# Three ring banks for the turned blocks of an attention stage, turns ahead of scores on TensorE, and the lambda rows taken last

## The chip, the cores and the metric

The kernel runs on one NeuronCore of one Trainium2 chip. The metric is the device time of one launch in microseconds (us), the median of several runs. Engines are named as in the profile: PE is TensorE, DVE is VectorE, ACT is ScalarE, POOL is GpSimd, and SP issues DMAs.

## The reference

One inference step of a two-layer hybrid backbone in float32, for 128 context tokens and 512 latent tokens. Each layer mixes tokens in three groups of heads (a gated DeltaNet, grouped-query attention, differential attention), projects the result, and runs a feed-forward part (dense in layer 0, a mixture of experts in layer 1). The change touches only the attention of the two layers:

```python
# B: 6 query heads, 2 key heads, 64 wide; latent queries see cached and latent keys, context queries see context keys
p = softmax(q_b @ k_b.T * HEAD_DIM ** -0.5);  o_b = p @ v_b
# C: 4 heads, two 32-wide softmax maps each, 64-wide values
p = softmax(q_c[m] @ k_c[m].T * DIFF_HD ** -0.5)          # m = 0, 1
lam = exp(sum(lv[0] * lv[1])) - exp(sum(lv[2] * lv[3])) + lam_init
o_c = rmsnorm((p[0] - lam * p[1]) @ v_c, diff_norm) * (1 - lam_init)
```

## The kernel before

The program is a row of stages; in each stage every engine has an instruction list written out by hand, and the engines meet at semaphores. At a stage's end all engines wait for one another. The change is in `attention`, called once for each of the two layers. It has two stages.

**The prepare stage** splits queries and keys into a high and a low part and transposes them, for seven items (five new tiles, two cached ones). For an item n, ACT writes the high parts (`split_hi`, L1567 to L1572), DVE the low parts (`split_lo`, L1518 to L1524), PE transposes them (L1602 to L1613), and ACT and DVE bring the results out of PSUM (`bring_out`). The rows of lambda, `lv`, arrive by SP's first DMA of the stage. DVE multiplies and sums them (L1539, L1540) before its first `split_lo`; ACT takes their exponential (L1588) after its first `split_hi`. Meanwhile POOL squares the DeltaNet output, five operations (L1503).

**The softmax stage** works through 14 units: six heads of kind B and four heads of kind C with two maps m = 0, 1 each. All loops over units are software-pipelined: iteration v issues work of unit v (`now`), of v+1 (`ahead`) and of v-1 (`done`). A unit has five query tiles t (tile 0 is the context). For each tile:

- **S**t: `scores` on PE into one of two pairs of banks (0 and 1, 2 and 3). Kind B takes four matmuls, kind C two, tile 0 a quarter of that.
- **least** on DVE (L1836, a reduction over the scores in PSUM), then **exp** on ACT (L1903, in the list `probabilities`), which frees the score banks for the scores after the next.

The probabilities are transposed in seven blocks (`ITEMS`), **T**0 to **T**6 (`turn`, L1743, four 128x128 transposes each, T3 only one). Each lands in a bank of the ring; ACT copies it out as the high part (**hi**j, L1913), DVE subtracts for the low part (**lo**j, L1841), and after that the bank is free. Then **W** (`weigh`, L1761) multiplies two key blocks by the values: W of the first half (tiles 1, 2) waits for lo2, that of the second half (tiles 3, 4) for lo6 and runs in the next iteration. **X** (`weigh_context`, L1772) does the context tile. ACT brings the sums out (L1921, L1923), **R** (`turn_out`, L1782) transposes them back on PE, and DVE scales them (**out**, L1847 to L1857; maps m = 1 have two more operations there than m = 0).

Waits that matter: S waits until exp has read the tile two before; T waits for lo of the block that last held its bank; W0 for lo2 or lo6; DVE does, in order, lo0, least1, lo1, least2, lo2, lo3, lo4, least3, lo5, least4, out, lo6, least0, and the change leaves this order and ACT's as they are in this stage. Before the change the PSUM banks are: ring 4 and 5, the sums in 6, and bank 7 for both X's result and R's result:

```python
RING, OB, XB = 4, 6, 7
def ring(n): return ps[:, RING + n % 2, :]
```

In layer 0 SP also fills 25 MB of slots with zeros during this stage.

Of the kernel before, what the change touches and what calls it, by code (L numbers as in the profile page):

```python
# [25 lines left out]
P = 128  # L26
# [129 lines left out]
class Kernel:  # L156
# [1264 lines left out]
    def attention(self, l):  # L1421
# [12 lines left out]
        with ExitStack() as scope:  # L1434
# [12 lines left out]
            with ExitStack() as inner:  # L1447
# [33 lines left out]
                with stage(nc, names) as (block, s):  # L1481
# [26 lines left out]
                    def _(dve):  # L1508
# [27 lines left out]

                        dve.wait_ge(s["lv_in"], 16)
# [3 lines left out]
                        for n in range(len(items)):  # L1541
                            split_lo(n)
                            if n:
                                bring_out(n - 1)
# [11 lines left out]
                    def _(act):  # L1556
# [30 lines left out]
                        act.wait_ge(s["lsum"], 1)  # L1587
                        act.activation(ls[:], ls[:], ACT.Exp).then_inc(s["lexp"], 1)  # L1588
# [3 lines left out]
                        bring_out(len(items) - 1)  # L1592

# [46 lines left out]
            RING, OB, XB = 4, 6, 7  # L1640
# [11 lines left out]
            def ring(n):  # L1652
                return ps[:, RING + n % 2, :]
# [11 lines left out]
            def turned(n):  # L1665
                size = len(ITEMS[n % NS])
                if size == 1:
                    return ring(n)[:, 0:P]
                return ring(n).rearrange("p (k q) -> p k q", k=4 if ITEMS[n % NS][0][1] == 0 else 2)
# [15 lines left out]
            with stage(nc, "folded v_hi v_lo scores least p_in turned hi lo pv pvc o_sb o_ctx o_turned o_out chain zeroed filled root inv gated") as (block, s):  # L1685
# [29 lines left out]
                def _(pe):  # L1715
# [21 lines left out]
                    def turn(u, j):  # L1737
                        n = NS * u + j
                        pe.wait_ge(s["p_in"], max(order(u, t) for t, k in ITEMS[j]) + 1)
                        if n >= 2:  # L1740
                            pe.wait_ge(s["lo"], n - 1)
                        for q, (t, k) in enumerate(ITEMS[j]):
                            mm = pe.transpose(ring(n)[:, q * P:(q + 1) * P], prob_block(u, t, k) if t else prob_slot(u, 0), self.ident)  # L1743
# [22 lines left out]
                    def weigh_context(u):  # L1766

                        pe.wait_ge(s["lo"], NS * u + 4)
                        if u:
                            pe.wait_ge(s["o_out"], u)  # L1770
                        for n, part in enumerate((p_hi, p_lo)):
                            mm = pe.matmul(ps[:, XB, 0:P], values(u, 0), part[:, PL:PL + P], start=(n == 0), stop=(n == 1))  # L1772
                        mm.then_inc(s["pvc"], 1)

                    def turn_out(u):
# [4 lines left out]
                        pe.wait_ge(s["o_ctx"], u + 1)  # L1780
                        for t in range(NT):
                            mm = pe.matmul(ps[:, XB, P + t * HD:P + (t + 1) * HD], oT[:, (t - 1) * P:t * P] if t else oTc, fold,  # L1782
                                           start=True, stop=True)
                        mm.then_inc(s["o_turned"], 1)
                    for v in range(-1, NU + 1):
                        ahead, now, done = v + 1 < NU, 0 <= v < NU, v >= 1
                        if ahead:
                            scores(v + 1, 1)
# [992 lines left out]
```

## Time and profile before

| | |
|---|---|
| median of 3 runs | 2812.03 us (2804.58 to 2816.2) |
| the profiled execution | 2805.11 us, of it the span of instructions 2803.4 us |
| busy in the span | PE 2426.6 us (87%), DVE 1450.3 us (52%), ACT 1068.4 us (38%) |
| prepare stage, layer 0 | 411.1 to 447.3 us |
| softmax stage, layer 0 | 447.3 to 652.1 us |
| softmax stage, layer 1 | 1617.7 to 1819.2 us |
| ACT's copies L1913, all 196: idle before them | 122.5 us, for PE's turns L1743 |
| DVE's subtractions L1841, all 196: idle before them | 117.9 us, for ACT's copies L1913 |

A row of a timeline gives the start in us, the duration in us, the engine, the line, the operation and its operands, how many instructions are merged in the row, and in brackets the idle time of the engine before it with what ended it. Two instructions of one engine overlap slightly in such rows, so what an instruction costs its engine in a full queue is the distance to the next start.

### The profile page before, as it was taken

How to read it: one execution, taken by the hardware profiler on the slowest of the kernel's cores; microseconds unless marked ns; L12 is line 12 of the kernel's file. 1: busy time of each engine (PE TensorE's matmuls, PEld its weight loads, DVE VectorE, ACT ScalarE, POOL GpSimd, SP SyncE). 2: the span in 40 equal slices, each digit the busy share in tenths (PEclk: the TensorE clock that was granted, in tenths of full speed). 3: DMA queues.
4: the chain of work that ended last, by engine and by line, in shares of the span. 5: the costliest groups of instructions: out<-in, count | busy, mean ns of one | idle time of the engine just before them, and what ended most of it. 6: DMA issues, size and time to landing. Idle time of an engine off the chain costs nothing. (4 is left out here: it accounts for less than half of the span.)

```text
span 2803.4 us, 47191 instructions
## 1 busy us (share of the span) xinstructions
PE 2426.6 (87%) x19308; PEld 2197.1 (78%) x19308; DVE 1450.3 (52%) x2079; ACT 1068.4 (38%) x1752; POOL 312.2 (11%) x334
## 2 busy tenths in 40 slices
PE   5996777877899999989958688784799999999993
PEld 4984555667899999989846656684799999999992
DVE  5576555575422322346746646642454555555456
ACT  4332235563422112243322456622344444444443
POOL 0055232000000000000643220001000000000002
PEclk8998887999999999999979889995899999999997
DMA  5233666502222322223157000011866676676654
GB/s 209 84 82 76 198 187 204 171 1 73 64 76 57 87 76 66 62 53 90 41 115 204 23 1 1 3 59 61 253 205 179 209 229 192 186 224 209 188 183 175
DMA packets 453116, 340.49 MB, mean 121 GB/s; under 512 B 90961, under 2 KB 421151, under 8 KB 451935
## 3 DMA queue, kind: packets, MB, share of 16 engines
q1 hardware_dynamic: 436383, 277.43, 34.3%
q10 hardware_dynamic: 11520, 41.95, 4.6%
q0 software_dynamic: 5056, 18.88, 1.7%
q8 instruction: 116, 1.90, 0.3%
q14 instruction: 41, 0.34, 0.0%
HBM read 287.68 MB, written 50.53 MB: 121 GB/s over the span
## 5 line engine op out<-in xcount | busy, mean ns | idle before, releaser
L2346 PE MATMUL ps<-h_hi,w_hi 128*128 128x256 f32 x1408 | 400.1, 284 | 5.5 <-DVE w_lo L2429 5.5
L2346 PE MATMUL ps<-h_lo,w_hi 128*128 128x256 f32 x1408 | 399.5, 284 | 0.0
L2346 PE MATMUL ps<-h_hi,w_lo 128*128 128x256 f32 x1408 | 399.5, 284 | 0.0
L2429 DVE TENSOR_TENSOR w_lo<-w_raw,w_hi 128x2048 fp32r<-128x2048 f32 (+1 forms) x180 | 309.2, 1756 | 120.5 <-ACT w_hi L2379 120.5
L2346 PEld LDWEIGHTS ps<-h_hi,w_hi 128*128 128x128 f32 x1408 | 271.2, 193 | 8.7 <-issue 5.9
L2346 PEld LDWEIGHTS ps<-h_lo,w_hi 128*128 128x128 f32 x1408 | 271.2, 193 | 2.8
L2346 PEld LDWEIGHTS ps<-h_hi,w_lo 128*128 128x128 f32 x1408 | 271.1, 193 | 0.0
L2379 ACT CAST w_hi<-w_raw 128x2048 fp32r<-128x2048 f32 (+1 forms) x180 | 256.4, 1473 | 2.6 <-DMA w_raw<-in_moe_w_down 2.6
L1841 DVE TENSOR_TENSOR p_lo<-ps,p_hi 128x512 fp32r<-128x512 f32 (+1 forms) x196 | 123.6, 632 | 123.0 <-ACT p_hi L1913 117.9
L2648 PE MATMUL ps<-ffn_h_hi,w_hi_ffn 128*128 128x320 f32 x704 | 161.5, 311 | 5.6 <-DVE ffn_h_lo L378 4.2
L2648 PE MATMUL ps<-ffn_h_lo,w_hi_ffn 128*128 128x320 f32 x704 | 160.9, 310 | 0.0
L2648 PE MATMUL ps<-ffn_h_hi,w_lo_ffn 128*128 128x320 f32 x704 | 160.9, 310 | 0.0
L2391 ACT ACTIVATE silu_g<-ps 128x256 f32<-128x256 f32 x88 | 33.8, 384 | 326.2 <-PE ps L2346 326.1
L1913 ACT CAST p_hi<-ps 128x512 fp32r<-128x512 f32 (+1 forms) x196 | 106.4, 544 | 122.5 <-PE ps L1743 122.5
L2439 DVE TENSOR_TENSOR silu_g<-silu_g,ps 128x256 f32<-128x256 f32 x88 | 37.0, 421 | 194.1 <-ACT silu_g L2391 194.1
L1743 PE MATMUL ps<-cst,tm 128*128 128x128 f32 x700 | 116.3, 287 | 12.0 <-DVE p_lo L1841 12.0
L596 PE MATMUL ps<-w_hi_in,h_hi 128*128 128x454 f32 x320 | 122.4, 382 | 4.6 <-DVE w_lo_in L152 3.1
L2648 PEld LDWEIGHTS ps<-ffn_h_hi,w_hi_ffn 128*128 128x128 f32 x704 | 118.4, 189 | 7.0 <-issue 6.7
L2092 DVE SCALAR_TENSOR_TENSOR xT<-ps,mod,xT 128x128 f32<-128x128 f32 (+2 forms) x96 | 36.3, 434 | 168.9 <-PE ps L2659 104.3
L1903 ACT ACTIVATE tm<-ps,tm 128x768 f32<-128x768 f32 (+1 forms) x140 | 111.7, 798 | 30.8 <-DVE tm L1836 30.8
L1836 DVE TENSOR_REDUCE tm<-ps 128x1 f32<-128x768 f32 (+1 forms) x140 | 114.0, 816 | 17.5 <-PE ps L1731 17.3
L596 PE MATMUL ps<-w_lo_in,h_hi 128*128 128x454 f32 x320 | 119.4, 373 | 0.0
(426 smaller groups left out, 5603.9 us busy)
## 6 DMA issues: line engine op xcount, KB each, us to landing
w_raw<-in_moe_w_gu SPq DMA_DIRECT2D x182, 512.0 KB
w_raw<-in_moe_w_down SPq DMA_DIRECT2D x91, 512.0 KB
G_decay<-in_ada_w ACTq DMA_DIRECT2D x54, 512.0 KB, 4.7
w_ahead<-in_ffn_w_gu SPq DMA_DIRECT2D x44, 512.0 KB, 5.3
slots_h<-tm SPq DMA_DIRECT2D x13, 1024.0 KB, 11.2
slots_y<-tm SPq DMA_DIRECT2D x12, 1024.0 KB, 11.4
w_ahead<-in_ffn_w_down SPq DMA_DIRECT2D x16, 704.0 KB, 4.7
oA<-in_ada_w ACTq DMA_DIRECT2D x20, 512.0 KB, 5.2
```

What stands on the lines that cost most here:

```text
L596: mm = pe.matmul(ps[:, t, 0:TMT], x[:, 4 * half + k, t * P:(t + 1) * P], wt[:, tile % 2, k * TMT:(k + 1) * TMT], start=(half == 0 and k == ...
L1743: mm = pe.transpose(ring(n)[:, q * P:(q + 1) * P], prob_block(u, t, k) if t else prob_slot(u, 0), self.ident)
L1836: dve.tensor_reduce(low[:, u % 2, t:t + 1], score_tile(u, t), AX.X, ALU.min).then_inc(s["least"], 1)
L1841: dve.tensor_tensor(place(p_lo, j), turned(n), place(p_hi, j).bitcast(F32), ALU.subtract).then_inc(s["lo"], 1)
L1903: act.activation(prob_slot(u, t), x.rearrange("p (a n) -> p a n", a=3) if t else x, ACT.Exp, scale=-1.0, bias=low[:, u % 2, t:t + 1], accu ...
L1913: act.copy(place(p_hi, j), turned(n)).then_inc(s["hi"], 1)
L2092: dve.scalar_tensor_tensor(out=x, in0=self.ps[:, 2 * (m % 4) + half, a - a0:b - a0], scalar=self.mod[:, l, gate, m, j:j + 1], in1=x, op0=A ...
L2346: mm = pe.matmul(ps[:, j % 2, half * BLK:(half + 1) * BLK], gu(wt, j, half, k), x[:, k, :], start=(k == 0 and n == 0), stop=(k == KC - 1 a ...
L2379: act.copy(whi[:, q, part], raw[:, q, part]).then_inc(s["hi_d" if down else "hi_u"], 1)
L2429: dve.tensor_tensor(wlo[:, q, part], raw[:, q, part], whi[:, q, part].bitcast(F32), ALU.subtract).then_inc(s["lo_d" if down else "lo_u"], 1)
L2439: dve.tensor_tensor(g, g, ps[:, j % 2, BLK:2 * BLK], ALU.mult).then_inc(s["prod"], 1)
L2648: mm = pe.matmul(ps[:, 4 * (j % 2) + 2 * half + st, 0:b - a], wt[:, u, o:o + P], x[:, k, a:b], start=(k == 0 and m == 0), stop=(k == KC - ...
```

## The change

In the prepare stage DVE's two products and the sum of the lambda rows move from the front of its list to behind the last `split_lo`, and ACT's exponential moves behind the last `bring_out`. In the softmax stage the ring has three banks (4, 5, 6), X's and R's results get no bank of their own but take turns in the ring, and the sums move to bank 7. The ring's order in a unit is T0, T1, T2, X, T3, T4, T5, R, T6 over the banks 0, 1, 2, 0, 1, 2, 0, 1, 2. On PE, S1 moves behind T0 and the W that follows it, S2 behind T2, S3 behind T4 and its W, and S4 behind R.

```diff
@@ prepare stage, DVE @@
+                        for n in range(len(items)):
+                            split_lo(n)
+                            if n:
+                                bring_out(n - 1)
                         dve.wait_ge(s["lv_in"], 16)
                         for j in range(2):
                             chain(dve.tensor_tensor(lp[:, j], lv[:, 2 * j], lv[:, 2 * j + 1], ALU.mult))
                         dve.tensor_reduce(ls[:], lp[:], AX.X, ALU.add).then_inc(s["lsum"], 1)
-                        for n in range(len(items)):
-                            split_lo(n)
-                            if n:
-                                bring_out(n - 1)
                         bring_out(len(items) - 1)
...
@@ prepare stage, ACT @@
                         split_hi(0)
-                        act.wait_ge(s["lsum"], 1)
-                        act.activation(ls[:], ls[:], ACT.Exp).then_inc(s["lexp"], 1)
                         for n in range(1, len(items)):
                             split_hi(n)
                             bring_out(n - 1)
                         bring_out(len(items) - 1)
+                        act.wait_ge(s["lsum"], 1)
+                        act.activation(ls[:], ls[:], ACT.Exp).then_inc(s["lexp"], 1)
...
@@ softmax stage @@
-            RING, OB, XB = 4, 6, 7
+            RING, OB = 4, 7
...
-            def ring(n):
-                return ps[:, RING + n % 2, :]
+            BANK = {0: 0, 1: 1, 2: 2, "context": 0, 3: 1, 4: 2, 5: 0, "result": 1, 6: 2}
+
+            def ring(j):
+                return ps[:, RING + BANK[j], :]
...
                     def turn(u, j):
-                        n = NS * u + j
                         pe.wait_ge(s["p_in"], max(order(u, t) for t, k in ITEMS[j]) + 1)
-                        if n >= 2:
-                            pe.wait_ge(s["lo"], n - 1)
+                        if j == 0 and u:
+                            pe.wait_ge(s["lo"], NS * (u - 1) + 6)
+                        elif j == 1 and u:
+                            pe.wait_ge(s["lo"], NS * (u - 1) + 4)
+                            if u >= 2:
+                                pe.wait_ge(s["o_out"], u - 1)
+                        elif j == 2 and u:
+                            pe.wait_ge(s["lo"], NS * u)
+                        elif j == 5:
+                            pe.wait_ge(s["lo"], NS * u + 1)
+                            if u:
+                                pe.wait_ge(s["o_ctx"], u)
+                        elif j >= 3:
+                            pe.wait_ge(s["lo"], NS * u + {3: 2, 4: 3, 6: 5}[j])
...
                     def weigh_context(u):
 
-                        pe.wait_ge(s["lo"], NS * u + 4)
-                        if u:
-                            pe.wait_ge(s["o_out"], u)
+                        pe.wait_ge(s["lo"], NS * (u + 1) + 1 if u + 1 < NU else NS * NU)
...
                         pe.wait_ge(s["o_ctx"], u + 1)
+                        if u + 1 < NU:
+                            pe.wait_ge(s["lo"], NS * (u + 1) + 4)
+                        else:
+                            pe.wait_ge(s["o_out"], u)
...
                     for v in range(-1, NU + 1):
                         ahead, now, done = v + 1 < NU, 0 <= v < NU, v >= 1
-                        if ahead:
-                            scores(v + 1, 1)
                         if now:
                             turn(v, 0)
                         if done:
                             weigh(v - 1, 1, 0)
                             weigh(v - 1, 1, 1)
+                        if ahead:
+                            scores(v + 1, 1)
                         if now:
                             turn(v, 1)
-                        if ahead:
-                            scores(v + 1, 2)
...
                             turn(v, 2)
+                        if ahead:
+                            scores(v + 1, 2)
...
                             turn(v, 3)
+                            turn(v, 4)
+                            weigh(v, 0, 0)
+                            weigh(v, 0, 1)
                         if ahead:
                             scores(v + 1, 3)
                         if now:
-                            turn(v, 4)
-                            weigh(v, 0, 0)
-                            weigh(v, 0, 1)
                             turn(v, 5)
-                        if ahead:
-                            scores(v + 1, 4)
-                        if now:
                             weigh(v, 0, 2)
                             weigh(v, 0, 3)
                         if done:
                             turn_out(v - 1)
+                        if ahead:
+                            scores(v + 1, 4)
```

Where PE's list passes from one unit of kind C to the next, before the change: S0 (128 keys), S1 (512 and 256 keys), T0 (the transposes of `cst,tm`), the first four matmuls W, T1.

```order
L1734 MATMUL ps<-kC,qC 128x128
L1734 MATMUL ps<-kC,qC 128x512
L1734 MATMUL ps<-kC,qC 128x256
L1743 MATMUL ps<-cst,tm 128x128 x4
L1761 MATMUL ps<-p_hi,vC 128x256
L1761 MATMUL ps<-p_lo,vC 128x256
L1761 MATMUL ps<-p_hi,vC 128x256
L1761 MATMUL ps<-p_lo,vC 128x256
L1743 MATMUL ps<-cst,tm 128x128 x4
```

The same place of PE's list in the changed kernel (the line numbers are its own):

```order
L1735 MATMUL ps<-kC,qC 128x128
L1755 MATMUL ps<-cst,tm 128x128 x4
L1773 MATMUL ps<-p_hi,vC 128x256
L1773 MATMUL ps<-p_lo,vC 128x256
L1773 MATMUL ps<-p_hi,vC 128x256
L1773 MATMUL ps<-p_lo,vC 128x256
L1735 MATMUL ps<-kC,qC 128x512
L1735 MATMUL ps<-kC,qC 128x256
L1755 MATMUL ps<-cst,tm 128x128 x4
```

S1 has moved behind T0 and the W whose first matmul waits for lo6 of the unit before.

PE's list from T5 to T6 in a unit of kind C, before the change: T5, S4, four matmuls W, R (x5), T6.

```order
L1743 MATMUL ps<-cst,tm 128x128 x4
L1734 MATMUL ps<-kC,qC 128x512
L1734 MATMUL ps<-kC,qC 128x256
L1761 MATMUL ps<-p_hi,vC 128x256
L1761 MATMUL ps<-p_lo,vC 128x256
L1761 MATMUL ps<-p_hi,vC 128x256
L1761 MATMUL ps<-p_lo,vC 128x256
L1782 MATMUL ps<-tm 128x64 x5
L1743 MATMUL ps<-cst,tm 128x128 x4
```

The same place in the changed kernel:

```order
L1755 MATMUL ps<-cst,tm 128x128 x4
L1773 MATMUL ps<-p_hi,vC 128x256
L1773 MATMUL ps<-p_lo,vC 128x256
L1773 MATMUL ps<-p_hi,vC 128x256
L1773 MATMUL ps<-p_lo,vC 128x256
L1796 MATMUL ps<-tm 128x64 x5
L1735 MATMUL ps<-kC,qC 128x512
L1735 MATMUL ps<-kC,qC 128x256
L1755 MATMUL ps<-cst,tm 128x128 x4
```

S4 has moved behind the W and behind R.

DVE's list at the start of the prepare stage, the change against before; `lp` and `ls` are the products and sums of lambda:

```order
 L1507 UNCONDITIONAL_BRANCH
-L1539 TENSOR_TENSOR lp<-lv 128x32 x2
-L1540 TENSOR_REDUCE ls<-lp 128x2
 L1518 TENSOR_TENSOR split_lB<-tm,split_kB 128x128
 L1522 TENSOR_TENSOR split_qB<-tm,split_qB 128x3x64 x2
```

`split_lo` of the first item now opens the list.

## Rows read from the trace of the kernel before

**Rows 1.** Windows: busy us of PE, PEld, DVE, ACT, POOL; PEclk, DMA share, GB/s

```profile
505.00:520.00 15.00, 13.44 (x79) 9.79 (x78) 8.59 (x14) 8.16 (x19) 0.00 (x0) 1.00 1.03 342
...
580.00:595.00 15.00, 12.38 (x91) 10.77 (x90) 12.15 (x20) 10.48 (x26) 0.00 (x0) 1.00 0.00 0
```

**Rows 2.** Timeline of PE, kind C: S1, T0, W, T1; R, T6

```profile
590.35 0.62 PE L1734 MATMUL ps<-kC,qC 96*128 96x512 f32 x2 [1.03 <-ACT tm L1903]
590.81 0.60 PE L1743 MATMUL ps<-cst,tm 128*128 128x128 f32 x4
591.16 0.36 PE L1761 MATMUL ps<-p_hi,vC 128*128 128x256 f32 x1
...
591.73 0.60 PE L1743 MATMUL ps<-cst,tm 128*128 128x128 f32 x4
...
599.12 1.22 PE L1782 MATMUL ps<-tm 128*128 128x64 f32 x10
600.18 0.61 PE L1743 MATMUL ps<-cst,tm 128*128 128x128 f32 x4
```

**Rows 3.** Timeline of ACT (exp of tile 4), DVE (least4, product of out; least4, lo6)

```profile
589.29 0.91 ACT L1903 ACTIVATE tm<-ps,tm 128x768 f32<-128x768 f32 x1
...
599.35 0.95 DVE L1836 TENSOR_REDUCE tm<-ps 128x1 f32<-128x768 f32 x1
...
600.45 0.49 DVE L1853 TENSOR_TENSOR oA<-ps,tm 128x320 f32<-128x320 f32 x1
...
611.35 0.95 DVE L1836 TENSOR_REDUCE tm<-ps 128x1 f32<-128x768 f32 x1
...
613.74 0.69 DVE L1841 TENSOR_TENSOR p_lo<-ps,p_hi 128x512 fp32r<-128x512 f32 x1
```

**Rows 4.** Timeline of PE, T4 of the last three units of layer 0

```profile
619.99 0.63 PE L1743 MATMUL ps<-cst,tm 128*128 128x128 f32 x4 [0.67 <-DVE p_lo L1841]
...
631.98 0.63 PE L1743 MATMUL ps<-cst,tm 128*128 128x128 f32 x4 [0.68 <-DVE p_lo L1841]
...
642.07 0.63 PE L1743 MATMUL ps<-cst,tm 128*128 128x128 f32 x4 [0.61 <-DVE p_lo L1841]
```

**Rows 5.** Timeline of PE, kind B: T4, first and last matmul of S2, T4

```profile
519.47 0.66 PE L1743 MATMUL ps<-cst,tm 128*128 128x128 f32 x4
...
530.17 0.49 PE L1730 MATMUL ps<-kB,qB 128*128 128x512 f32 x1
...
531.33 0.38 PE L1731 MATMUL ps<-kB_lo,qB 64*128 64x256 f32 x1
...
534.82 0.66 PE L1743 MATMUL ps<-cst,tm 128*128 128x128 f32 x4
```

**Rows 6.** Timeline at the start of layer 0's prepare stage

```profile
411.10 3.96 POOL L1503 TENSOR_TENSOR mixed<-oA 128x384 f32<-128x384 f32 x5 [3.68 <-POOLq L84]
411.40 0.60 ACT L1570 CAST split_qB<-tm 128x192 fp32r<-128x192 f32 x2
...
415.62 0.28 DVE L1518 TENSOR_TENSOR split_lB<-tm,split_kB 128x128 fp32r<-128x128 f32 x1
...
416.50 1.54 PE L1602 MATMUL ps<-cst,split_qB 128*128 128x128 f32 x6 [7.96 <-DVE split_qB L1522]
```

**Rows 7.** Source L1539: min/median/max ns, first and last start; what ended its waits

```profile
L1539 DVE TENSOR_TENSOR lp<-lv x4: 191/192/580, 415.0 to 1585.6; 128x32 f32<-128x32 f32 x4
...
  DMA lv<-in_diff_lambda: 9.5, 2
```

**Rows 8.** Timeline of DVE, its last copy from PSUM in the prepare stage

```profile
442.86 0.69 DVE L1535 CAST kC<-ps 96x512 fp32r<-96x512 f32 x1 [1.19 <-PE ps L1613]
```

**Rows 9.** Timeline of PE, T4 of the first three units of layer 0

```profile
470.72 1.11 PE L1743 MATMUL ps<-cst,tm 128*128 128x128 f32 x4
...
485.46 0.66 PE L1743 MATMUL ps<-cst,tm 128*128 128x128 f32 x4
...
504.14 0.65 PE L1743 MATMUL ps<-cst,tm 128*128 128x128 f32 x4
```

More of the change, by code:

```diff
@@ L1663, in place, with turned @@
                 return grid[:, 4:6, :]
[L1665 to L1669, printed above, removed]
+            def turned(j):
+                if len(ITEMS[j]) == 1:
+                    return ring(j)[:, 0:P]
+                return ring(j).rearrange("p (k q) -> p k q", k=4 if ITEMS[j][0][1] == 0 else 2)
             def score_tile(u, t):
@@ L1737, in turn @@
                     def turn(u, j):
-                        n = NS * u + j
                         pe.wait_ge(s["p_in"], max(order(u, t) for t, k in ITEMS[j]) + 1)
-                        if n >= 2:
-                            pe.wait_ge(s["lo"], n - 1)
+                        if j == 0 and u:
[12 more added lines that the diff above has]
+                            pe.wait_ge(s["lo"], NS * u + {3: 2, 4: 3, 6: 5}[j])
                         for q, (t, k) in enumerate(ITEMS[j]):
-                            mm = pe.transpose(ring(n)[:, q * P:(q + 1) * P], prob_block(u, t, k) if t else prob_slot(u, 0), self.ident)
+                            mm = pe.transpose(ring(j)[:, q * P:(q + 1) * P], prob_block(u, t, k) if t else prob_slot(u, 0), self.ident)
                         mm.then_inc(s["turned"], 1)
@@ L1766, in weigh_context @@
                     def weigh_context(u):
-                        pe.wait_ge(s["lo"], NS * u + 4)
-                        if u:
-                            pe.wait_ge(s["o_out"], u)
+                        pe.wait_ge(s["lo"], NS * (u + 1) + 1 if u + 1 < NU else NS * NU)
                         for n, part in enumerate((p_hi, p_lo)):
-                            mm = pe.matmul(ps[:, XB, 0:P], values(u, 0), part[:, PL:PL + P], start=(n == 0), stop=(n == 1))
+                            mm = pe.matmul(ring("context")[:, 0:P], values(u, 0), part[:, PL:PL + P], start=(n == 0), stop=(n == 1))
                         mm.then_inc(s["pvc"], 1)
@@ L1780, in turn_out @@
                         pe.wait_ge(s["o_ctx"], u + 1)
+                        if u + 1 < NU:
+                            pe.wait_ge(s["lo"], NS * (u + 1) + 4)
+                        else:
+                            pe.wait_ge(s["o_out"], u)
                         for t in range(NT):
-                            mm = pe.matmul(ps[:, XB, P + t * HD:P + (t + 1) * HD], oT[:, (t - 1) * P:t * P] if t else oTc, fold,
+                            mm = pe.matmul(ring("result")[:, t * HD:(t + 1) * HD], oT[:, (t - 1) * P:t * P] if t else oTc, fold,
                                            start=True, stop=True)
@@ L1840, in split_lo @@
                         dve.wait_ge(s["hi"], n + 1)
-                        dve.tensor_tensor(place(p_lo, j), turned(n), place(p_hi, j).bitcast(F32), ALU.subtract).then_inc(s["lo"], 1)
+                        dve.tensor_tensor(place(p_lo, j), turned(j), place(p_hi, j).bitcast(F32), ALU.subtract).then_inc(s["lo"], 1)
                     def out(u):
@@ L1850, in out @@
                         dve.wait_ge(s["o_turned"], u + 1)
-                        po = ps[:, XB, P:P + NT * HD].rearrange("p (t d) -> p t d", d=HD)
+                        po = ring("result")[:, 0:NT * HD].rearrange("p (t d) -> p t d", d=HD)
                         dst = mixed[:, :, AW + h * HD:AW + (h + 1) * HD] if kind == "B" else oc1[:] if m else oC[:, :, h]
@@ L1912, in split_hi @@
                             act.wait_ge(s["pvc"], u)
-                        act.copy(place(p_hi, j), turned(n)).then_inc(s["hi"], 1)
+                        act.copy(place(p_hi, j), turned(j)).then_inc(s["hi"], 1)
                     def bring_out(u):
@@ L1922, in bring_out @@
                         act.wait_ge(s["pvc"], u + 1)
-                        act.copy(oTc, ps[:, XB, 0:P]).then_inc(s["o_ctx"], 1)
+                        act.copy(oTc, ring("context")[:, 0:P]).then_inc(s["o_ctx"], 1)
                     act.activation(ro[:], ro[:], ACT.Sqrt).then_inc(s["root"], 1)
```

## The prediction, made blind

> **What bounds the kernel now.** I read the windows first. In a stretch of kind B TensorE is busy 13.44 of 15 us at the full clock, in one of kind C 12.38 of 15, beside DVE with 12.15 and ACT with 10.48 [rows 1]. So no engine is full in C, and in B TensorE nearly is: what sets the time there is a ring of waits, and the timeline shows which. T4 comes every 11.99 us in C (619.99 to 631.98 [rows 4]) and every 15.35 us in B (519.47 to 534.82 [rows 5]). TensorE idles 1.03 us before S1, for ACT's exp of tile 4 [rows 2]: exp starts at 589.29 [rows 3], S1 at 590.35, so 1.06 us from the start of an exp to the scores that it lets go. T0 stands behind S1 in the list, so ACT has no block to copy meanwhile. It idles again for 0.67 us before T4, for lo2 [rows 4]. The old ring is T4, hi4, exp2, S4, W, R, T6, hi6, exp4, S1, T0, hi0, exp0, S2, and so on.
>
> To test my way of adding, I walked this old order by distances between starts: from T4 0.63 (its length) to hi4, 0.49 to exp2, 1.05 to S4, and so on round; it closes after 12.07 us in C, where the trace has 11.99, and in B it meets each row within 0.1 us. (0.49 is ACT's step from one copy to the next.) The new order is walked in the same way.
>
> **The softmax stage, step by step (C).** Distances in TensorE's full queue: W of four matmuls 0.57 (591.16 to 591.73), a turn of four 0.35, S 0.46 (590.35 to 590.81), R 1.06 (599.12 to 600.18) [rows 2]. From a start to its reader: S lasts 0.62, so least starts 0.65 after S; a T that waits for lo starts 0.84 after lo (0.69 long, plus the 0.15 seen between engines). DVE spends 0.86 on least. From least4 to lo6 in a full queue it takes 2.39 us for m = 1 (611.35 to 613.74); for m = 0, 1.10 to the product (599.35 to 600.45) and about 0.42 more, a little under its 0.49, so 1.52 [rows 3].
>
> With S4 behind R and S1 behind W, whose first matmul waits for lo6, the ring after the change is: T4, W, S3, T5, W, R, 3.37 us to S4; 0.65 to least4; 1.52 to lo6 (2.39 when m = 1); 0.84 to W; then W 0.57, S1 0.46, T1 0.36, W 0.57, T2 0.36 to S2; 0.65 to least2; 0.86 to lo2, which stands behind least2 on DVE; 0.84 to T4. Sum 11.05 us, or 11.92 with m = 1. All else has slack: exp4 lets S1 go 0.9 us before W is through, hi2 ends 0.16 before lo2 can start, and TensorE waits 1.1 us before this W and 1.1 before T4. So the gain of three banks and of T0 ahead of S1 (T0 now runs 1.5 us before lo6's W) is largely given back, since S4, and with it least4, out and lo6, comes 1.2 us later than before (3.37 us after T4 against 0.63 + 0.49 + 1.05 = 2.17), and W for lo6 blocks S1 in the queue.
>
> In layer 0 seven such rings lie between the T4 of units 5 and 12; in two of them R belongs to a map m = 1. Gain: 5 x 0.94 + 2 x 0.07 = 4.9 us. The last one, without scores ahead, took 10.09 us before (631.98 to 642.07 [rows 4]). Its R belongs to m = 1; before, W for lo6 was at 6.50 us from T4 there, in the new walk it comes at 7.25: a loss of 0.75. Behind it nothing changes.
>
> **Kind B.** S has four matmuls, 1.16 us from first to last start and 0.38 for the last (530.17, 531.33 [rows 5]), so 1.54 long and 1.47 in the queue. The same ring: 4.45 to S4, 1.57 to least4, 1.52 to lo6, 0.84 to W, 0.56 + 1.47 + 0.40 + 0.56 + 0.35 to S2, 1.57, 0.86, 0.84: 14.99 us against 15.35. Three rings in each layer: 1.1 us. The one from B to C comes to 13.05 against 13.13: 0.1.
>
> **The start.** For unit 0, T4 used to stand behind S3. With T0 ahead of S1 and S3 behind T4, the walk at half clock has T4 2.0 us earlier than the 470.72 of [rows 9]. The next ring, which had 14.74 us (470.72 to 485.46), has no R and takes 15.0: net 1.65 us. I leave the clock as it is: it was 0.5 until 473 us and again from 491 to 501, and the second spell made a B ring take 18.68 us (485.46 to 504.14 [rows 9]) where 15.35 is usual, so 3.3 us, once, in layer 0 alone. It may go or move.
>
> **The other edits of this stage.** The new waits of X (lo0), T1 (out of two units before), T5 (X brought out) and R (lo3) all end over 0.5 us before TensorE comes there in both walks: nothing. If that cover went, each would hold TensorE's whole list. Merging X's bank into the ring puts nothing in ACT's list or DVE's. SP's zero fill runs on no path.
>
> **The prepare stage.** Before, DVE waited for lambda's rows (9.5 us in both layers [rows 7]), and TensorE's first transpose came at 416.50, 0.88 us after the first `split_lo` at 415.62. ACT's high parts are ready at 412.00 (411.40 + 0.60 [rows 6]). So TensorE could start at 412.9, 3.6 us earlier, and all seven items follow, for they are one chain over ACT, TensorE and DVE. ACT gets rid of its exponential in front of item 1. What is moved costs nothing at the new place: the three DVE operations (0.19 each, 0.22) fit in the 1.19 us that DVE idles before its last copy [rows 8], and the exponential lies beside DVE's reduction that follows. If that cover were gone it would be 0.7 us.
> But POOL squares from 411.10 to 415.06 [rows 6], with operands in SBUF as `split_lo` has them, and DVE's products of lambda show what that may do: 0.19 us typically, 0.58 for the one that began during a square [rows 7]. The bounds are then no hold (3.6) and a hold until the last square ends (0.6). I take 2.1, two holds of about 0.7, since a held operation was freed when the running square ended.
> The Trainium skill (SBUF — State Buffer, "SBUF: two separate sides") says of the port pair that DVE and GpSimd share that whoever starts first gets it for the whole instruction, and names DVE operations with two SBUF inputs against a GpSimd operation that reads SBUF. The 0.58 us agrees. If the three operations and the squares took turns by that rule, the gain would be 1.3 us a layer and the sum 16.5 instead of 18.
>
> **The sum.** A layer: 2.1 + 1.65 + 1.1 + 0.1 + 4.9 - 0.75 = 9.1 us; two layers 18. Behind the attention the stages start their own loads, so all of it shifts. The profiled execution would go from 2805.1 to 2787 us. It lay 7 us under the median of the runs shown, so against the median: 2812 - 18 = 2794 us. Bounds: the start of the prepare stage is off by 1.5 us a layer either way, and the walk, which rests on a few steps not seen (scores right behind a turn, DVE's 0.42), by up to 0.5 us in each of 11 rings: together 7 us a layer. So gains of 4 to 32 us, times of 2780 to 2808. A change of under 0.5%, 14 us, can hardly be told from none in this kernel.
>
> **Rivals.**
> *The chain loses what it gains.* If scores behind a turn cost 0.25 us more, or the copies of ACT join the ring (hi2 has only 0.16 us of slack), C rings take 11.6 to 12.0 us. Then the prepare stage and the start are what is left: 2 to 12 us, about 2805. For it: the slack is thin and S4 is late by my own count. Against it: the test walk closed within 0.1 us.
> *Three banks decouple the engines.* If the wait for lo6 lay elsewhere than I think, TensorE's own queue would bound: 8.9 us for C and 13.1 for B (my sums of its distances), 3.1 us and 2.2 us less a ring, over 28 us a layer, about 2750. Against it: DVE's list alone needs 8.3 to 9.2 us in C, and lo6 stands behind least4 and out in a list that is unchanged.
> *Slower: the clock falls.* The new list makes TensorE wait twice a C ring for 1.1 us. If the clock fell to half for it, TensorE's 8.9 us of work would become about 16, 5 us more than 11 a ring; with four such rings in all the gain is gone, with ten the kernel is 32 us slower than before, 2844. Against it: the clock was 1.00 with 0.97, 0.67 and like waits in every C ring [rows 1, 4], and in the new order TensorE's share of a ring rises. The Trainium skill (TensorE: Matmul & The Clock Gate, "A second HAM failure mode: psum-queue depth-cycling") reports a kernel whose clock did swing because TensorE idled briefly and often between groups. Here it did not in C before; the spell from 491 us came in B, with TensorE busy.
>
> **How the numbers follow.** My forecast, a gain of 12 to 25 us, 0.60, of which 0.50 is over 14; the chain that loses its gain 0.25; decoupled banks 0.08; slower by the clock or otherwise, from no gain on, 0.07, of which 0.04 is over 14 us. So faster by over 0.5% 0.58, within 0.5% 0.38, slower 0.04. The range 2780 to 2808 holds the first case whole and most of the second.
>
> **What would show it.** The first transpose of the prepare stage at 413 to 415 us, with `split_lo` operations longer than 0.28 and 0.35 where squares run. T4 every 11.05 us in C, 11.9 where R belongs to m = 1. TensorE's waits in C before W for lo6 and before T4, both for DVE, and none left for ACT before S1. DVE idle between lo5 and least4. The prediction is wrong if T4 comes at 11.6 or more with W waiting elsewhere, or if the clock row of a C window is under 1.

## The result: 2816.2 to 2792.1 us, ratio 0.9917

The changed kernel takes 2792.09 us (median of 6 runs, 2784.98 to 2793.17), the kernel before on the same chip 2816.18 us (6 runs, 2804.58 to 2818.48). The ratio is 0.9917, with a 95% interval of 0.9898 to 0.9937: a small gain, clear of none. The profiled execution took 2791.23 us, with a span of 2789.6 us; that of before lay 11 us under its own median, so the two profiles differ by only 13.8 us where the medians differ by 24.

Windows of the changed kernel (columns as in [rows 1]): kind B, kind C of layer 0, and one in C of layer 1.

```profile
505.00:520.00 15.00, 13.94 (x84) 10.42 (x84) 9.13 (x15) 8.51 (x21) 0.00 (x0) 1.00 1.04 342
580.00:595.00 15.00, 11.44 (x92) 10.59 (x91) 12.46 (x23) 10.77 (x26) 0.00 (x0) 1.00 0.01 2
1740.00:1750.00 10.00, 7.29 (x46) 6.71 (x45) 6.59 (x14) 5.97 (x15) 0.00 (x0) 0.83 0.01 2
```

In B TensorE is fuller than in [rows 1]. In C no engine is full, as before, and in the third window the granted clock (PEclk) is under 1.

Timeline of PE in one ring of kind C with m = 0: T4, S3, S4, W that waits for lo6, S1, T1, S2; behind the dots the same W one unit later, where R belongs to m = 1, and the next two T4.

```profile
564.75 0.63 PE L1755 MATMUL ps<-cst,tm 128*128 128x128 f32 x4 [0.95 <-DVE p_lo L1854]
...
565.70 0.51 PE L1735 MATMUL ps<-kC,qC 96*128 96x512 f32 x2
...
568.00 0.60 PE L1735 MATMUL ps<-kC,qC 96*128 96x512 f32 x2
...
570.86 0.38 PE L1773 MATMUL ps<-p_hi,vC 128*128 128x256 f32 x1 [0.83 <-DVE p_lo L1854]
...
571.44 0.51 PE L1735 MATMUL ps<-kC,qC 96*128 96x512 f32 x2
571.78 0.60 PE L1755 MATMUL ps<-cst,tm 128*128 128x128 f32 x4
...
573.06 0.60 PE L1735 MATMUL ps<-kC,qC 96*128 96x512 f32 x2
...
582.42 0.38 PE L1773 MATMUL ps<-p_hi,vC 128*128 128x256 f32 x1 [1.76 <-DVE p_lo L1854]
...
586.96 0.63 PE L1755 MATMUL ps<-cst,tm 128*128 128x128 f32 x4 [0.96 <-DVE p_lo L1854]
...
597.61 0.63 PE L1755 MATMUL ps<-cst,tm 128*128 128x128 f32 x4 [0.95 <-DVE p_lo L1854]
```

T4 comes every 10.65 us (586.96 to 597.61), where [rows 4] had 11.99. TensorE now waits in two places, before W and before T4, both for DVE's `p_lo`; the wait for ACT's exp before S1 [rows 2] is gone. The same ring on DVE: least4, product, lo6, then least2 and lo2.

```profile
568.63 0.96 DVE L1849 TENSOR_REDUCE tm<-ps 128x1 f32<-128x768 f32 x1 [0.44 <-PE ps L1735]
...
569.72 0.49 DVE L1866 TENSOR_TENSOR oA<-ps,tm 128x320 f32<-128x320 f32 x1
570.12 0.68 DVE L1854 TENSOR_TENSOR p_lo<-ps,p_hi 128x512 fp32r<-128x512 f32 x1
...
573.69 0.96 DVE L1849 TENSOR_REDUCE tm<-ps 128x1 f32<-128x768 f32 x1
574.57 1.02 DVE L1854 TENSOR_TENSOR p_lo<-ps,p_hi 128x512 fp32r<-128x512 f32 x2
```

The start of the prepare stage, timelines of POOL, DVE and PE, answering to [rows 6], and T4 of the first three units, answering to [rows 9]:

```profile
411.86 4.24 POOL L1503 TENSOR_TENSOR mixed<-oA 128x384 f32<-128x384 f32 x5 [3.58 <-POOLq L84]
...
412.79 0.82 DVE L1518 TENSOR_TENSOR split_lB<-tm,split_kB 128x128 fp32r<-128x128 f32 x1 [2.03 <-ACT split_qB L1570]
413.54 1.87 DVE L1522 TENSOR_TENSOR split_qB<-tm,split_qB 128x192 fp32r<-128x192 f32 x2
...
415.47 1.54 PE L1602 MATMUL ps<-cst,split_qB 128*128 128x128 f32 x6 [6.18 <-DVE split_qB L1522]
...
466.44 1.09 PE L1755 MATMUL ps<-cst,tm 128*128 128x128 f32 x4 [1.34 <-DVE p_lo L1854]
...
486.78 0.63 PE L1755 MATMUL ps<-cst,tm 128*128 128x128 f32 x4 [0.76 <-DVE p_lo L1854]
...
501.44 0.63 PE L1755 MATMUL ps<-cst,tm 128*128 128x128 f32 x4 [0.76 <-DVE p_lo L1854]
```

The first transpose stands 3.6 us behind the stage's first operation (415.47 - 411.85), before it was 5.4 us behind (416.50 - 411.09). The first ring took 20.3 us (466.44 to 486.78) against 14.7.

Where the time went, us won in each layer, by distances between the same marks of the two traces:

| term | forecast | layer 0 | layer 1 |
|---|---|---|---|
| prepare stage, up to the first score | 2.1 | 2.9 | 2.0 |
| first score to T4 of unit 0 | 2.0 | 2.15 | 2.15 |
| first ring | -0.3 | -5.6 | -5.8 |
| three B rings | 1.1 | 5.4 | 2.0 |
| ring from B to C | 0.1 | 0.5 | 0.5 |
| seven C rings | 4.9 | 7.6 | 4.5 |
| last ring | -0.75 | -0.5 | -1.6 |
| sum | 9.1 | 12.5 | 3.8 |

3.3 us of layer 0's 5.4 are the spell of low clock in the ring of 18.68 us [rows 9], which did not come back. The two sums make 16.3 us. The profiles differ by 13.8 us in all, for everything outside the attention took some 2 us more in the changed kernel's profile.

### The profile page after: what moved, and what is told of

Its sections match the earlier page's. It is cut to its first block and busy times, and to the rows that moved or that the text cites. A ratio compares the mean times of both kernels' runs of the same rounds, so it can differ in the third digit from the quotient of the medians.

```text
span 2789.6 us, 47165 instructions
## 1 busy us (share of the span) xinstructions
PE 2423.0 (87%) x19308; PEld 2202.9 (79%) x19308; DVE 1459.6 (52%) x2079; ACT 1069.0 (38%) x1752; POOL 313.0 (11%) x334
## 5 line engine op out<-in xcount | busy, mean ns | idle before, releaser
L1755 PE MATMUL ps<-cst,tm 128*128 128x128 f32 x700 | 123.2, 298 | 24.8 <-DVE p_lo L1854 24.8
L596 PE MATMUL ps<-w_hi_in,h_lo 128*128 128x454 f32 x320 | 118.5, 370 | 0.0
## 6 DMA issues: line engine op xcount, KB each, us to landing
slots_y<-tm SPq DMA_DIRECT2D x12, 1024.0 KB, 11.2
```

Of the source, the lines that this page charges most:

```text
L596: mm = pe.matmul(ps[:, t, 0:TMT], x[:, 4 * half + k, t * P:(t + 1) * P], wt[:, tile % 2, k * TMT:(k + 1) * TMT], start=(half == 0 and k == ...
L1755: mm = pe.transpose(ring(j)[:, q * P:(q + 1) * P], prob_block(u, t, k) if t else prob_slot(u, 0), self.ident)
```

## The experiments

Each kernel was timed beside the kernel before. "Ratio" is to the kernel before, with its 95% interval. Times in us are compared with the changed kernel's 2792.09 us across sessions, in which the kernel before itself had medians of 2813.39 to 2816.37 us; so a difference of a few us between two kernels means little.

**The lambda rows alone.** The kernel before with only the prepare-stage part of the change's diff.

> The kernel before with the late lambda rows alone; ring, banks and TensorE's order stay as they were. My theory: the prepare stage gains what the changed kernel's trace shows, some 1.7 to 1.8 us until TensorE's first transpose and up to 1 us more where the clock rises during item 0, so 2 to 3 us in each layer: 4 to 6 us under before, T4 every 12.0 us in C rings and the low clock at the start of the softmax stage for 26 us as before. Rival (the lambda rows carry little, all of the gain is in the order): under 1.5 us.

Measured: 2814.05 us, ratio 1.0008 (0.9992 to 1.0024; 12 runs against 23). In the profile the first transpose came at +3.6 us in both layers, as in the changed kernel. C rings stayed at 12.00. The forecast of 4 to 6 us under before missed, and the total is the rival's. The stage gives 1.7 us a layer, and none of it is seen in the total: 3.5 us would be 0.12%, while the interval's lower end is 0.08% under 1. What gave it back is not shown by the runs. In its one profile low clock is a candidate: B rings of 16.5, 17.9 and 16.5 us in layer 1, with low clock in each, where before has 15.35.

**The ring part alone.** The changed kernel with the lambda rows back at the front.

> The changed kernel with the lambda rows taken early again, so the ring with three banks and the new order alone. My theory: the changed kernel plus 4 to 6 us, and in the trace again T4 every 10.65 us in C rings (11.57 where m = 1) and a low clock that lasts 39 us from the start of each softmax stage. Rival (the longer spell of low clock comes from the shifted start of the stage, not from the new order): here the low clock lasts 26 us as before, and the kernel is as fast as the changed one or faster.

Measured: 2798.62 us, ratio 0.9947 (0.9926 to 0.9967). C rings 10.65, as in the changed kernel. First rings 21.3 in both layers, with the clock at 0.5 for 45 us from the first score, so the longer spell does not come from the earlier start of the stage. The median is 6.5 us over the changed kernel's, but the intervals overlap.

**The new order with two banks.** The kernel before with late lambda rows and the changed kernel's order on TensorE; ring, X and R keep their old banks.

```diff
@@ kernel before, order of the changed one @@
                         if now:
                             turn(v, 0)
                         if done:
                             weigh(v - 1, 1, 0)
                             weigh(v - 1, 1, 1)
+                        if ahead:
+                            scores(v + 1, 1)
...
```

> The new order of TensorE and the late lambda rows on the old banks: a ring of two, the sums in bank 6, X and R in bank 7. My theory (the order does it all; no wait of the two-bank ring ends last in the new order, since T4 waits for lo2 in either): the time of the changed kernel within 3 us, C rings of 10.65 and 11.57 us. Rival (the third bank is what lets T0 go early): C rings near 12 us, and the time of the lambda rows alone, 15 us or more above the changed kernel.

**The three banks with the old order.** The changed kernel with the loop over v of the kernel before.

> Three banks and the late lambda rows with TensorE's old order. My theory (banks do nothing): the time of the lambda rows alone within 3 us, C rings of 12.0 us, low clock for 26 us. Rival (the banks carry a part of the gain): C rings of 11.5 us or less, and 6 us or more under the lambda rows alone.

Measured: the order alone 2788.9 us, ratio 0.9919 (0.9896 to 0.9943); the banks alone 2813.81 us, ratio 1.0002 (0.9987 to 1.0018). PE's T4 in kind C, first the order alone, then the banks alone:

```profile
557.81 0.63 PE L1743 MATMUL ps<-cst,tm 128*128 128x128 f32 x4 [0.95 <-DVE p_lo L1840]
...
568.45 0.63 PE L1743 MATMUL ps<-cst,tm 128*128 128x128 f32 x4 [0.95 <-DVE p_lo L1840]
```
```profile
571.79 0.63 PE L1755 MATMUL ps<-cst,tm 128*128 128x128 f32 x4 [0.67 <-DVE p_lo L1855]
...
583.79 0.41 PE L1755 MATMUL ps<-cst,tm 128*128 128x128 f32 x2 [0.67 <-DVE p_lo L1855]
```

10.65 and 12.00 us. Both forecasts held for the rings. The times lie 3.2 us under the changed kernel's and 0.2 us under that of the lambda rows alone, where 3 us either way were forecast; only the 26 us of low clock did not come with the banks alone, where it lasted 43 us in layer 0 and 31 in layer 1 from the first score. What the change gains in the softmax stage is the order's; the third bank does nothing. In either ring T4 waits for lo2, since X takes one of the slots that the third bank adds.

**lo6 ahead of out.** The changed kernel, on DVE alone.

```diff
-                        if done:
-                            if v - 1 == HB:
-                                dve.wait_ge(s["gated"], 3 * NT)
-                            out(v - 1)
                         if now:
                             split_lo(v, 6)
                         if ahead:
                             least(v + 1, 0)
+                        if done:
+                            if v - 1 == HB:
+                                dve.wait_ge(s["gated"], 3 * NT)
+                            out(v - 1)
```

> The changed kernel with one swap in DVE's list: lo6 and least0 ahead of out. My theory (out stands in the ring between least4 and lo6): walked with the distances of the changed kernel's trace, the C ring falls from 10.65 to 10.3 us and from 11.57 to 11.2 where m = 1, and TensorE's wait for lo6 is 0.9 us in both; 4 to 6 us under the changed kernel. Rival (lo6 is late because of hi6 and T6, not of out): rings as in the changed kernel, no gain.

Measured: 2781.46 us, ratio 0.988 (0.985 to 0.9909); C rings 10.30, with m = 1 11.20; B rings 14.40. PE's timeline, T4 and the waiting W:

```profile
596.98 0.63 PE L1755 MATMUL ps<-cst,tm 128*128 128x128 f32 x4 [1.04 <-DVE p_lo L1854]
602.65 0.39 PE L1773 MATMUL ps<-p_hi,vC 128*128 128x256 f32 x1 [0.41 <-DVE p_lo L1854]
608.17 0.63 PE L1755 MATMUL ps<-cst,tm 128*128 128x128 f32 x4 [1.33 <-DVE p_lo L1854]
```

The rings are as forecast. W's wait falls to 0.41 for either map, where 0.9 was forecast, and the median is 10.6 us under the changed kernel's, where 4 to 6 were; the two intervals just overlap. That lo6 stood behind out was part of the ring.

**TensorE kept busy ahead of the stage.** Twenty matmuls into a free bank behind the last transposes of each prepare stage, at PE's idle time before the first score.

```diff
                             mm.then_inc(s["turned_c"], 1)
+                        for _ in range(20):
+                            pe.matmul(ps[:, 7, :], sqB[:, 0, 0].rearrange("p u d -> p (u d)"),
+                                      sqB[:, 0, 0:4].rearrange("p h u d -> p (h u d)"), start=True, stop=True)
```

> The changed kernel with 20 more matmuls (512 columns, into bank 7, their result unused) at the end of TensorE's list of the prepare stage, some 4.3 us at the full clock, which cover the idle stretch before the softmax stage. My theory (the low clock of the first units is entered in that idle stretch, and the first units then leave it late): the clock stays at the full level into the softmax stage, T4 of unit 0 comes 3 us or more earlier and the first ring takes about 15 instead of 20.5 us: 10 to 18 us under the changed kernel. Rival (the first units, with their sparse scores, bring the clock down anyway): the clock falls within 10 us of the stage's start, and the gain is under 3 us.

Measured: 2793.54 us, ratio 0.9914 (0.9887 to 0.9941), no different from the changed kernel. Its windows:

```profile
441.00:446.00 5.00, 4.12 (x11) 1.99 (x10) 2.24 (x4) 4.92 (x10) 1.36 (x3) 0.86 0.79 263
446.00:476.00 30.00, 27.13 (x77) 17.56 (x77) 11.45 (x17) 12.37 (x28) 19.34 (x19) 0.50 1.04 343
```

The scores began at the full clock, at 440.55, and 4.1 us later it was down to 0.5, with TensorE busy 4.12 of 5 us; in layer 1 it fell 2.3 us after the first score. T4 of unit 0 came 0.7 us earlier, not 3, and the first rings took 20.6 and 18.3 us. The idle time ahead of the stage does not cause the spell, and the outcome is the rival's.

**The first unit in the old order.** The changed kernel, but iterations v = -1 and 0 issue TensorE's work in the order of the kernel before.

```diff
+                        if v <= 0:
+                            if ahead:
+                                scores(v + 1, 1)
+                            if now:
+                                turn(v, 0)
...
+                        else:
```

> The changed kernel with TensorE's old order for the first unit alone (scores ahead of turns up to unit 0), the new order from unit 1 on. If the new order of the first unit is what holds the clock low for longer at the start of the softmax stage, the spell is some 27 us again instead of 41 and the first ring takes 15 instead of 20.5 us; T4 of unit 0 comes 2.15 us later; in sum 4 to 8 us under the changed kernel. Rival (the length of the spell is chance, as the runs with the old order had 27 to 44 us): spells of any length from 27 to 44 us, and a time within 4 us of the changed kernel.

Measured: 2785.32 us, ratio 0.9887 (0.986 to 0.9914). The first rings take 15.2 and 15.7 us, with T4 of unit 0 at 23.4 us from the first score as before. The clock was low for 31.3 and 32.3 us from the first score, less than the 38 and 39 of the changed kernel but not the forecast's 27. The time is 7 us under the changed kernel's median, but the intervals overlap.

**R behind T6 as well.** The kernel of lo6 ahead of out, with S4 and T6 also ahead of R on PE.

```diff
-                        if done:
-                            turn_out(v - 1)
                         if ahead:
                             scores(v + 1, 4)
                         if now:
                             turn(v, 6)
                             weigh(v, 0, 4)
                             weigh(v, 0, 5)
+                        if done:
+                            turn_out(v - 1)
```

> As the run with lo6 ahead of out, and on TensorE S4, T6 and its W ahead of R. My theory (S4 behind R is what gave back the gain): least4 and lo6 come some 1 us earlier, C rings of 9.8 us and 10.7 where m = 1, B rings of 14.0 us; 12 to 20 us under the changed kernel. Rival (ACT and DVE are full by then): C rings of 10.3 us or more, and under 8 us gained.

Measured: 2768.15 us, ratio 0.9818 (0.9792 to 0.9845). C rings 9.95, with m = 1 10.63; B 14.10; the last ring 9.33. PE's waits of a C ring:

```profile
590.49 0.63 PE L1755 MATMUL ps<-cst,tm 128*128 128x128 f32 x4 [1.23 <-DVE p_lo L1854]
...
601.12 0.63 PE L1755 MATMUL ps<-cst,tm 128*128 128x128 f32 x4 [1.32 <-DVE p_lo L1854]
...
611.07 0.63 PE L1755 MATMUL ps<-cst,tm 128*128 128x128 f32 x4 [1.23 <-DVE p_lo L1854]
```

W no longer waits for lo6 at all. The forecast was 12 to 20 us under the changed kernel, and the median is 24 under it; this interval (0.9792 to 0.9845) lies wholly under the changed kernel's. By the distances of the two profiles, the B, C and last rings at the full clock are worth some 17 us of it (an estimate); the rest can be spells of low clock that no longer come (see below), which is not shown.

**POOL's squares later.** The changed kernel with one wait added ahead of POOL's five squares.

```diff
+                        pool.wait_ge(s["lo"], 4)
                         for t in range(NT):
                             pool.tensor_tensor(mixed[:, t, 0:AW], self.oA[:, t], self.oA[:, t], ALU.mult).then_inc(s["squared"], 1)
```

> The changed kernel; GpSimd's five squares of the prepare stage start only when VectorE has done the four low-part subtractions of the first two items (one wait added). Theory (the two engines get in each other's way): in the changed kernel those VectorE operations took 0.82 us (split_lB, 0.28 in the kernel before) and 1.87 us (the two split_qB, 0.62 before), while the squares ran beside them; without squares beside them they go back to 0.28 and 0.62, and the first transpose comes at about +1.9 us after the stage's first operation instead of +3.62. The squares themselves end about 2 us later than now, their results are wanted last and cover this. First scores up to 1.7 us earlier in each layer, the whole time 0 to 4 us under the changed kernel's. Rival (the operations are slow for a reason of their own, the input's arrival or a cold engine): they keep 0.82 and 1.87, the first transpose stays within 0.3 us of +3.62, and nothing is won.

Measured: DVE's and PE's timeline:

```profile
412.44 0.29 DVE L1519 TENSOR_TENSOR split_lB<-tm,split_kB 128x128 fp32r<-128x128 f32 x1 [2.03 <-ACT split_qB L1571]
412.65 0.62 DVE L1523 TENSOR_TENSOR split_qB<-tm,split_qB 128x192 fp32r<-128x192 f32 x2
...
413.33 1.54 PE L1603 MATMUL ps<-cst,split_qB 128*128 128x128 f32 x6 [4.39 <-DVE split_qB L1523]
```

The same operations take 0.29 and 0.62 us instead of 0.82 and 1.87, and the first transpose comes at +1.83. The squares take 3.96 us for five again instead of 4.24. So the two engines do hold each other up. The first scores came 0.7 us (layer 0) and 1.8 us (layer 1) sooner after the stage's first operation than in the changed kernel. Yet the whole time is 2793.51 us, ratio 0.9934 (0.9913 to 0.9954), that of the changed kernel: the gain did not arrive. In this profile every C ring with m = 1 took 13.15 us with a spell of low clock, four in all at 1.6 us each; the changed kernel's profile has two of them.

**Everything together.** R behind T6, with the first unit in the old order; and the same with the squares later.

> e8_result_last with the first unit of each attention stage in the kernel before's TensorE order. Theory (the long first ring is the sum of the new order and the low clock, and e7 took it back): T4 of the first unit at +23.4 after the first score as in the kernel before (+21.2 now), the first ring about 15.3 instead of 20.6 and 21.3, so 3 us a layer; later rings as in e8 (14.1, 9.95, 10.6). Whole time 3 to 8 us under e8's 2768, some 2762. Rival (how long the low clock lasts at the start is chance and not the order's doing): within 3 us of e8.

> e10 with the squares held back as in e9_squares_later. If the gain of e9 in the stage carries to the end: 1 to 4 us under e10, and a ratio to the kernel before of about 0.979. If what is won there is eaten by the low clock at the start of the attention, as with the lambda part alone: within 1 us of e10.

Measured: 2766.88 us, ratio 0.9837 (0.9819 to 0.9855), and 2762.77 us, ratio 0.9816 (0.9797 to 0.9835). First rings of 15.2 to 15.6 us in all four layers, as forecast, all later rings as in the kernel with R behind T6. But neither kernel can be told from that one by its time, nor from the other, so the forecasts of 3 to 8 and 1 to 4 us are not borne out by the times. In the profiles the gain is there: from the prepare stage's first high part to T4 of the last unit, the two layers together took 458.7 us in the kernel before, 442.5 in the changed one, 424.2 with R behind T6, and 416.6 and 410.3 in these two. All the rest of the program, which none of the edits touches, took 2338 to 2351 us in the profiles of the thirteen kernels. Against such differences between single executions, 7 us do not show. By their medians the three are 24 to 29 us faster than the changed kernel, and 1.6 to 1.8% faster than the kernel before.

## Why the prediction was right, and where its terms were off

**The sum.** Forecast 2794, measured 2792.1; as a ratio 0.9936 against 0.9917 (0.9898 to 0.9937). The mechanism held: the gain is the shorter ring, in B and C alike, and both remaining waits are for lo6 and lo2 (0.83 and 0.95 us, forecast 1.1 each). Part of the nearness is luck. The rings at the full clock gained more than the walk said (some 4 us a layer more, an estimate from the distances below), and the start lost 3.4 and 3.6 us a layer where 1.65 were to be won. The forecast also spoke of a "gain of three banks and of T0 ahead of S1"; with the order alone and the banks alone the banks' share is nothing. And one of its own signs of being wrong came true: a C window of layer 1 has a clock of 0.83.

**The C and B rings** were too long in the walk by 0.40 and 0.33 us: 10.65, 11.57 (m = 1), 14.67 and 12.66 (B to C) against 11.05, 11.92, 14.99 and 13.05. The term that was mis-sized is S3 and S1 in their new place right behind W. The walk took S as 0.46 in the queue; S1 is 0.51 long there, not 0.62, and T1 starts 0.34 behind it (571.44 to 571.78). So S4 comes 3.25 us after T4 (564.75 to 568.00) instead of 3.37, and T1 0.92 after W (570.86 to 571.78) instead of 1.03. Another 0.10 was the step from lo6 to W, 0.74 (570.12 to 570.86) instead of 0.84, and the rest is of some hundredths each. The walk was made new with these distances for the kernels that followed, and met their C rings within 0.15 us: 10.30 and 11.20 for 10.3 and 11.2, then 9.95 and 10.63 for 9.8 and 10.7.

**The late S4** was argued rightly: with lo6 ahead of out, and then with S4, T6 and its W ahead of R, the C ring gets 0.35 us and another 0.35 us shorter (0.37 and 0.57 where m = 1). What the change gave back by the longer way to lo6 was there to be taken.

**The start** failed as a step, the one that read "I leave the clock as it is". T4 of unit 0 did come 2.15 us earlier (2.0 in the forecast), but the first ring took 20.3 and 20.7 us, not 15.0. The clock stayed at 0.5 for 38 and 39 us from the first score, before 26 us. Over all profiles the first ring took 17.9 to 21.3 us in the fourteen layers with the new order in unit 0, and 14.7 to 16.6 in eleven of twelve layers with the old one (the twelfth 20.8). From the first score to T4 of unit 1 that is 41.1 us on average against 39.2, a loss of 1.9 us a layer where 1.65 us were to be won. Two things add up. At the same length of low clock the gain is already gone: 32.2 us of it with the old order in unit 0 (R behind T6 with the first unit old, layer 0) gave T4 of unit 1 at 39.0 us, 32.6 us of it with the new order (two banks, layer 1) at 39.1, since the earlier T4 puts more of the first ring under the low clock. And the spells were longer with the new order in unit 0: 32.6 to 44.9 us in its fourteen layers, 31.2 to 32.3 in the six where only unit 0 had the old one, though 26.0 to 42.7 in the six with the old order throughout. Busy matmuls ahead of the stage don't change it. Why the spell lasts so long, and why the order should matter to it, stays open: TensorE was busy 93% of the low spell in the changed kernel and 91% in the kernel before.

Windows of the two, inside the spell, the kernel before first:

```profile
448.00:472.00 24.00, 21.74 (x49) 12.10 (x49) 8.45 (x13) 12.06 (x26) 18.84 (x20) 0.50 0.99 330
```
```profile
445.00:480.00 35.00, 32.41 (x83) 19.78 (x83) 13.52 (x20) 17.89 (x37) 20.97 (x22) 0.50 0.98 325
```

**The prepare stage** gave 1.8 and 1.7 us at the first transpose, between my 2.1 and the 1.3 of the rule. The term of two holds was a little too small: three operations were held before that transpose, by 0.54 us and twice 0.62. The fourth, of the kind `split_kC`, took 1.04 us instead of 0.42. The holds were gone once the squares waited. The Trainium skill (SBUF — State Buffer, "SBUF: two separate sides") says that of the two engines the one that starts first has the shared port pair for its whole instruction. The trace agrees: 0.82 against 0.28, 1.87 against 0.62, and POOL's own operations longer too, 4.24 us for five against 3.96. That the stage's gain passes to the total is not shown: in the two kernels that isolate such a gain (the lambda rows alone, the squares later) it is not to be found. The moved operations cost nothing, as forecast: DVE idles 0.61 us before its last copy out of PSUM even with them there.

**The rival of the falling clock** came true in a small form, without making the kernel slower; the forecast had "slower" at 0.07. It was not brought by the two waits in every C ring, but came in rings with a wait of 1.76 us. PE's timeline in layer 1, behind such a wait:

```profile
1742.44 0.39 PE L1773 MATMUL ps<-p_hi,vC 128*128 128x256 f32 x1 [1.76 <-DVE p_lo L1854]
...
1743.02 0.81 PE L1735 MATMUL ps<-kC,qC 96*128 96x512 f32 x2
1743.63 1.06 PE L1755 MATMUL ps<-cst,tm 128*128 128x128 f32 x4
...
1746.67 0.28 PE L1773 MATMUL ps<-p_hi,vC 128*128 128x256 f32 x1
```

The granted clock is 0.5 from 1743.05 to 1746.46: S takes 0.81 us instead of 0.51 and T1 1.06 instead of 0.60, and the ring takes 13.16 instead of 11.57. Of the 24 rings with R of m = 1 in the profiles of the six kernels that have the 1.76 us wait, 17 took 12.5 to 13.2 us, the others 11.6. The last rings of these kernels have the wait too, and five of twelve were 1.1 to 1.3 us longer than the rest. In all 22 cases the clock fell 0.3 to 1.5 us after the start of the W that had waited, and nowhere else in a C ring of any profile. In the four kernels where this wait is gone and the longest is 1.33 us, none of 16 is longer than 11.2. Nor did the clock fall in the C rings of the old order, where TensorE idled nearly as long in all (2.5 us of 12.00, against 2.7 of 11.57) in waits of up to 1.03 us. The Trainium skill (TensorE: Matmul & The Clock Gate, "A second HAM failure mode: psum-queue depth-cycling") reports a clock that swings where TensorE idles briefly between groups; here it swung behind single waits of 1.76 us, at 1 to 1.6 us for each fall. It is not shown that the length of a wait decides it: in B rings of the old order the clock fell six times, in three of six layers, where no wait was over 0.79 us. In layer 1 of the changed kernel it took 3.2 us of the seven C rings' gain and 1.1 us of the last ring.

**The rival of the decoupled banks** is settled by the three banks with the old order: 12.00 us a ring, so no decoupling at all. **The rival of the lost gain** missed: C rings of 11.6 us or more came only with R of m = 1 and mostly with low clock, and the waits that are left in the ring are for DVE.

**Open.** The profiles' attention stages differ by 16 us, the medians by 24. The runs of the kernel before spread over 14 us, and low-clock spells in its B rings would be part of it. They come in profiles of the old order (3.3 us in [rows 9], 4.9 us in three rings with the lambda rows alone, some 8 us in two rings with the banks alone). With the new order only the spell from the start reaches into the second ring, at a cost of 1.0 to 1.1 us, in four of its fourteen layers. That was seen in single profiles only.

## What to carry to other kernels

Walk the ring of waits by distances between starts before adding banks: here the third bank was worth nothing, and the order in one engine's list everything. When something blocking moves ahead in a list, look at what now stands behind it and at what its reader does first: putting lo6 ahead of out and R behind T6 brought another 24 us. And look at TensorE's longest single wait in each ring as well as at their sum: here rings with one wait of 1.76 us often lost 1 to 1.6 us more to the clock. Last, a gain of 1 to 3 us a layer at a stage's start can be plain in a profile and still not show in the total.

## What the runs showed of the hardware

- In C rings a wait of 1.76 us was followed by a fall of the clock from 1.0 to 0.5 in 22 of 36 cases (17 of 24, and 5 of 12 in the last ring). C rings whose longest wait was 1.33 us or less never had one. B rings of the old order had six, with no wait over 0.79 us.
- At the start of the softmax stage the clock fell to 0.5 at 4.1 us (layer 0) and 2.3 us (layer 1) after the first score even when TensorE came to it busy and at the full clock. In all profiles it rose again 26 to 45 us after the first score, with TensorE busy for 90 to 95% of the low stretch from the first score on.
- A DVE subtraction with both operands in SBUF took 0.82 us instead of 0.28 beside GpSimd's squares, and two that take 0.62 together took 1.87.
